# Fetched rows on partitions 32 to 127 and slots that count downwards in half of the experts, in a two-layer encoder kernel

## What is computed

```python
D_MODEL = 1024
SEQ = 256
TOP_K = 2
EXPERT_FF = 3584

def moe_swiglu(x, w_router, b_router, w1, w3, w2):
    logits = jnp.dot(t, w_router) + b_router
    top_val, top_idx = lax.top_k(logits, TOP_K)
    top_w = jax.nn.softmax(top_val, axis=-1)
    gates = jnp.sum(jax.nn.one_hot(top_idx, N_EXPERTS) * top_w[..., None], axis=1)
    for e in range(N_EXPERTS):
        he = jax.nn.silu(t @ w1[e]) * (t @ w3[e])
        out = out + gates[:, e:e + 1] * (he @ w2[e])
```

## Time and profile before

| | |
|---|---|
| median of 3 runs | 1235.1 us (1233.23 to 1238.87) |
| the profiled execution | 1235.46 us |
| its span from first to last instruction | 1233.7 us |
| granted TensorE clock, mean | 0.992 |
| TensorE busy | 93% of the span |
| bytes moved | 421.58 MB, 342 GB/s over the span |

### The profile page before, as it was taken

How to read it: one execution, slowest core, us unless ns; L and a number is a source line. 1 busy time by engine, 2 the same in 40 slices (tenths; PEclk the granted TensorE clock), 3 DMA queues, 4 the chain that set the end, 5 groups by cost and what they waited for, 6 DMA issues and landing times.

```text
span 1233.7 us, 27683 instructions
## 1 busy us (share of the span) xinstructions
PE 1149.4 (93%) x12516; PEld 682.6 (55%) x12517; DVE 325.1 (26%) x546; ACT 262.0 (21%) x402; POOL 89.8 (7%) x131
## 2 busy tenths in 40 slices
PE   8999999999999999999999978899997789999784
PEld 7888888888985446445346423334642343354232
DVE  6977766767974010000000000000100000010000
ACT  6885244345751100000000000000000000000000
POOL 5303200000001000101000100100010010001000
PEclk9999999999999999999999989999999999999998
DMA  7559565662189999999999999999999999999992
GB/s 257 191 171 331 183 202 178 197 188 85 61 311 416 421 419 376 390 405 421 425 412 423 412 408 426 419 426 410 426 410 411 427 421 421 410 425 412 427 418 95
DMA packets 75080, 421.58 MB, mean 342 GB/s; under 512 B 5906, under 2 KB 42383, under 8 KB 50384
## 3 DMA queue, kind: packets, MB, share of 16 engines
q1 hardware_dynamic: 70000, 413.16, 83.4%
q0 software_dynamic: 4960, 6.61, 2.2%
HBM read 416.54 MB, written 4.72 MB: 341 GB/s over the span
## 4 chain that ended last, share of the span: by engine, by line
PE 69%; DMA 26%; DVE 2%; ACT 1%; issue 1%; POOL 0%; POOLq 0%; SPq 0%; DVEq 0%; ACTq 0%
PE ps L1283 26%; DMA w_ring<-in_moe_w_dram 25%; PE ps L1306 14%; PE ps L1020 7%; PE ps L737 5%; PE ps L739 5%; PE ps L738 5%; PE ps L1025 3%; PE ps L1296 1%; DMA residual<-in_x_dram 0%; PE ps L858 0%; PE ps L1267 0%; POOL head_rstd L617 0%; PE ps L939 0%; PE ps L1176 0%
## 5 line engine op out<-in xcount | busy, mean ns | idle before, releaser
L1283 PE MATMUL ps<-w_ring,expert_in 128*32 128x512 f32 (+1 forms) x5120 | 496.1, 544 | 44.4 <-DMA w_ring<-in_moe_w_dram 44.4
L1283 PEld LDWEIGHTS ps<-w_ring,expert_in 128*32 128x32 f32 x5120 | 176.0, 111 | 356.2 <-issue 277.5
L1306 PE MATMUL ps<-w_ring,expert_hT 128*32 128x256 f32 x4480 | 248.7, 380 | 17.5 <-DMA w_ring<-in_moe_w_dram 17.5
L1306 PEld LDWEIGHTS ps<-w_ring,expert_hT 128*32 128x32 f32 x4480 | 144.0, 110 | 116.7 <-DMA w_ring<-in_moe_w_dram 26.5
L1790 DVE TENSOR_TENSOR w_lo<-w_raw,w_hi 128x2048 fp32r<-128x2048 f32 (+2 forms) x63 | 127.5, 2050 | 35.1 <-ACT w_hi L1367 35.0
L1020 PE MATMUL ps<-act_both,w_hi 128*128 128x512 f32 x352 | 122.4, 396 | 0.0
L1367 ACT ACTIVATE w_hi<-w_raw 128x2048 fp32r<-128x2048 f32 (+2 forms) x62 | 104.2, 1717 | 3.1 <-DMA w_raw<-in_mla_w_kvb_dram 2.4
L2351 DVE TENSOR_TENSOR expert_h<-expert_h,ps 128x896 f32<-128x896 f32 x20 | 21.8, 1088 | 301.9 <-PE ps L1283 301.8
L1025 PE MATMUL ps<-act_both,w_lo 128*128 128x256 f32 x352 | 91.4, 280 | 0.0
L1753 ACT ACTIVATE expert_hT<-ps 128x896 f32<-128x896 f32 x20 | 17.7, 916 | 284.3 <-PE ps L1296 284.3
L698 POOL DMA_INDIRECT out_dram<-expert_out,slot_row x20 | 31.1, 1554 | 592.4 <-ACT expert_out L1769 588.8
(11 more groups left out here) (357 smaller groups left out, 986.4 us busy)
## 6 DMA issues: line engine op xcount, KB each, us to landing
w_ring<-in_moe_w_dram SPq DMA_DIRECT2D x192, 1792.0 KB, 42.1
w_raw<-in_ffn_w_dram SPq DMA_DIRECT2D x33, 1024.0 KB, 5.3
w_raw<-in_lru_w_in_dram SPq DMA_DIRECT2D x8, 1024.0 KB, 5.4
w_raw<-in_mla_w_o_dram SPq DMA_DIRECT2D x4, 1024.0 KB, 5.0
w_raw<-in_lru_w_out_dram SPq DMA_DIRECT2D x4, 1024.0 KB, 5.0
w_raw<-in_mla_w_in_dram SPq DMA_DIRECT2D x8, 352.0 KB, 7.3
w_raw<-in_mla_w_qb_dram SPq DMA_DIRECT2D x4, 576.0 KB, 3.9
w_raw<-in_mla_w_kvb_dram SPq DMA_DIRECT2D x2, 1024.0 KB, 12.5
```

The costliest lines, as they stand in the source:

```text
L1283: ins = pe.matmul(ps[j * STRIP:(j + 1) * STRIP, 2 * g + b, 0:wide], in_x[:, c, k, g * STRIP:(g + 1) * STRIP], w[:, j * PART + at:j * PART ...
L1306: return pe.matmul(ps[j * STRIP:(j + 1) * STRIP, bank, at:at + DOWN_COLS], hT[:, a:a + STRIP], w, start=first and at == 0, stop=last and ( ...
```

## The change

Three things are changed.

1. The fetch has 128 rows and writes partitions 32 to 127. Partitions 0 to 31 get an offset of 1024, so their rows are out of bounds. The transposes of TensorE then have 128 rows and columns, and `take_in` reads the last 96 columns of each 128. `pick_slots` fills the token numbers with four calls rather than three, one strip further down.
2. `slot_ids` has a second version, in which the numbers of each group of 32 count downwards: 31 to 0, 63 to 32, 95 to 64. `FALLING` picks it for places 1, 2, 5 and 6. There the first token of a group sits on the last partition of a strip, for the fetch and for the adds.
3. GpSimd makes the second version and the offsets with one more iota and two more memsets.

```diff
+    FALLING = [0, 1, 1, 0, 0, 1, 1, 0]
...
-    slot_ids = sbuf.take("slot_ids", [P, CAP])
+    slot_ids = sbuf.take("slot_ids", [P, 2, CAP])
...
+            own.step(pool.iota(slot_ids[:, 1, :].rearrange("p (g t) -> p g t", g=GROUPS),
+                               pattern=[[STRIP, GROUPS], [-1, STRIP]], base=STRIP - 1, channel_multiplier=0,
+                               allow_small_or_imprecise_dtypes=True))
...
+            own.link(pool.memset(token_of[:], float(NOWHERE)))
+            own.link(pool.memset(token_of[0:STRIP, :], 2.0 * NOWHERE))
...
-                pool.indirect_dma_start(fetched_x[0:CAP, :], None, normed,
-                                        bass.IndirectOffsetOnAxis(ap=slot_token[0:CAP, c:c + 1], axis=0),
+                pool.indirect_dma_start(fetched_x[:], None, normed,
+                                        bass.IndirectOffsetOnAxis(ap=slot_token[:, c:c + 1], axis=0),
...
-                    for g in range(GROUPS):
-                        pick(g, g, SEQ + 2 * GROUPS)
+                    for j in range(STRIPS):
+                        pick(j, max(j - 1, 0), SEQ + 2 * GROUPS)
...
-                        ins = pe.transpose(ps[:, 4 + k // 4, k % 4 * CAP:(k % 4 + 1) * CAP], fetched_x[0:CAP, k * P:(k + 1) * P],
-                                           ident[0:CAP, 0:CAP])
+                        ins = pe.transpose(ps[:, 4 + k // 4, k % 4 * P:(k % 4 + 1) * P], fetched_x[:, k * P:(k + 1) * P], ident[:])
...
-                act.activation(in_x[:, c, 0:4, :], ps[:, 4, 0:4 * CAP].rearrange("p (k t) -> p k t", k=4),
+                act.activation(in_x[:, c, 0:4, :], ps[:, 4, :].rearrange("p (k t) -> p k t", k=4)[:, :, P - CAP:P],
...
-                        ins = dve.tensor_scalar(sel[:, c, i, :], slot_ids[:], sorted_rank[:, i, column(SORTED_AT[e])], None,
+                        ins = dve.tensor_scalar(sel[:, c, i, :], slot_ids[:, FALLING[e], :], sorted_rank[:, i, column(SORTED_AT[e])], None,
...
-                dve.tensor_scalar(slot_token[0:CAP, c:c + 1], ps[0:CAP, 7, at + 1:at + 2], float(NOWHERE), None,
+                dve.tensor_scalar(slot_token[:, c:c + 1], ps[:, 7, at + 1:at + 2], token_of[:, 0:1], None,
```

More of the change, by code:

```diff
@@ L240, in encoder_trunk @@
     strip_of = sbuf.take("strip_of", [P, 1])
+    token_of = sbuf.take("token_of", [P, 1])
     slot_gate = sbuf.take("slot_gate", [P, 2, GROUPS])
@@ L598, in _ @@
             own.step(pool.memset(mask[0:P // 2, P // 2:P], NEG))
-            own.step(pool.iota(slot_ids[:], pattern=[[1, CAP]], base=0, channel_multiplier=0,
+            own.step(pool.iota(slot_ids[:, 0, :], pattern=[[1, CAP]], base=0, channel_multiplier=0,
+                               allow_small_or_imprecise_dtypes=True))
+            own.step(pool.iota(slot_ids[:, 1, :].rearrange("p (g t) -> p g t", g=GROUPS),
+                               pattern=[[STRIP, GROUPS], [-1, STRIP]], base=STRIP - 1, channel_multiplier=0,
                                allow_small_or_imprecise_dtypes=True))
@@ L1213, in gather @@
                     for i in range(TT):
-                        ins = pe.matmul(ps[:, 4 + k // 4, k % 4 * CAP:(k % 4 + 1) * CAP], rx[:, i, k * P:(k + 1) * P],
+                        ins = pe.matmul(ps[:, 4 + k // 4, (k % 4 + 1) * P - CAP:(k % 4 + 1) * P], rx[:, i, k * P:(k + 1) * P],
                                         sel[:, 0, i, :], start=k % 4 == 0 and i == 0, stop=k % 4 == 3 and i == TT - 1)
@@ L2295, in _ @@
             for i in range(TT):
-                dve.tensor_scalar(sel[:, 0, i, :], slot_ids[:], rank[:, i, 0:1], None, ALU.is_equal).then_inc(sel_ready, 1)
+                dve.tensor_scalar(sel[:, 0, i, :], slot_ids[:, FALLING[0], :], rank[:, i, 0:1], None, ALU.is_equal).then_inc(sel_ready, 1)
             dve.wait_ge(top_exp, 1)
@@ L2314, in take_in @@
                 dve.tensor_copy(in_x[:, c, 4:KD, :],
-                                ps[:, 5, 0:4 * CAP].rearrange("p (k t) -> p k t", k=4)).then_inc(in_dve, 1)
+                                ps[:, 5, :].rearrange("p (k t) -> p k t", k=4)[:, :, P - CAP:P]).then_inc(in_dve, 1)
             def select(e, c, shift):
@@ L2320, in select @@
                     if shift is False:
-                        ins = dve.tensor_scalar(sel[:, c, i, :], slot_ids[:], sorted_rank[:, i, column(SORTED_AT[e])], None,
+                        ins = dve.tensor_scalar(sel[:, c, i, :], slot_ids[:, FALLING[e], :], sorted_rank[:, i, column(SORTED_AT[e])], None,
                                                 ALU.is_equal)
                     else:
-                        ins = dve.tensor_scalar(sel[:, c, i, :], slot_ids[:], top_off[:, shift], rank[:, i, column(e)],
+                        ins = dve.tensor_scalar(sel[:, c, i, :], slot_ids[:, 0, :], top_off[:, shift], rank[:, i, column(e)],
                                                 ALU.add, ALU.is_equal)
```

## The result

The changed kernel takes **1228.61 us** (median of 6 runs, 1227.14 to 1230.61) against 1235.52 us before (6 runs beside them, 1233.23 to 1239.01). The ratio is 0.9934, 95% interval 0.9920 to 0.9948, so the gain is clear and above the 0.5% that can be told. The medians differ by 6.9 us; the ratio stands for 8.2 us (6.4 to 9.9). The forecast of 1233.2 us and its range from 1229.7 us were too high. The profiled execution took 1227.14 us, its span is 1225.3 us, 8.4 us shorter than before.

What follows compares the result with a forecast made beforehand. The weight stream through full DMA engines was taken to set the end. Levelling -2.4, entries +0.2 and transposes +0.3 us made -1.9 us, giving 1233.2 us against 1235.1; range 1229.7 to 1238.2 us.

Steps and rivals of the forecast that it cites:

- What bounds the kernel: Expert part: after 507 us the DMA engines are full and the weight stream sets the end; 376 to 427 GB/s.
- 32 more entries per fetch: Each fetch: two more out-of-bounds entries per engine move no data; 0.2 us taken, between 0 and 1.2 us.
- Levelling: End of the stream: fetched rows and adds spread more evenly over DMA engines; -2.4 us taken, bounds 0 and -3.9 us.
- Levelling of the fetched rows: Seven fetches: surplus of the most loaded engine falls from 2.1 to 0.4 us; -1.7 us.
- Transposes: TensorE: 56 transposes grow to 128 x 128; 2.0 us if uncovered, mostly hidden by waits, 0.3 us taken.
- Landing and constants: A fetch landing one us later, and GpSimd's extra iota and two memsets, cost nothing.
- 1 (no change): End of the stream: slow engines are not those with many rows, only costs remain; 1235.6 us, chance 0.16.
- 2 (1226.6 us): End of the stream: small transfers are the whole cause, nearly all 10.0 us idle time goes; 1226.6 us, chance 0.07.
- 3 (the highest slots meet the slowest engine): Adds: downward counting gives the last-ending engine up to 32 more, 2.8 us; 1238.4 us, chance 0.08.
- 4 (runs of eight): Shifted fetches: shares are runs of eight, so engines 4 to 7 get 56 rows, 2.1 us more; 1237.0 us, chance 0.09.
- What would make the prediction wrong: Changed profile: end idle time stays 10.0 us, grows or shrinks to 1 or 2; `fetched_rows` waits; GB/s falls between fetches.

Runs made afterwards that it cites:

- experiment 4: Kernel before with 32 out-of-bounds entries behind the 96 of each fetch, rows on partitions 0 to 95, all slots counting upwards: 1228.23 us, ratio 0.9936.
- 5: Experiment 4 with fetches of 112 entries in place of 128: 1234.88 us, ratio 0.9986 against the kernel before.
- 6: Kernel before with fetches of 64 entries in the four places of two groups, 96 in the others: 1236.34 us, ratio 1.0000.
- experiment 1: Changed kernel with all slots counting upwards, still 128 entries and partitions 32 to 127: 1230.62 us, ratio 0.9948 against the kernel before.

## Why the prediction was wrong, point by point

- **What bounds the kernel**: right, but for the last slice, whose 95 GB/s is outside the 376 to 427 that were read. The stream sets the end, and what it gained came off the time.
- **The step that failed** is in "32 more entries per fetch": "That loss falls on all engines and comes from the rows moved, which stay the same in number." The loss was seen (366 GB/s against 427) and its cause asserted. It hangs on whether the fetch has 128 entries. With the same rows moved and 32 empty entries behind them the loss goes (experiment 4), with 16 it stays (5), and with fewer entries it is no larger (6). Its price was in the rows: 61 of 427 GB/s over 6 to 7 us is 1 us per fetch, 6 to 7 us in all. The forecast had no term for it. Two readings should have raised doubt. GB/s already holds the fetched bytes, so moving rows lowers nothing. And the adds, of 128 entries and 1024 bytes each, lose less (406) than a fetch of 96 entries of 4096 bytes. That the time still went down while the levelling brought next to nothing is the work of a term that the forecast didn't have.
- **32 more entries at 0.2 us**: no cost can be seen. A fetch of 128 costs 0.6 us, which is what its bytes take.
- **Levelling, -2.4 us**: too large, and not shown to be more than nothing. The idle time at the end fell by 0.9 us (1.6 us in the second profile), but it scatters by 0.7 us in one kernel. The direction alone gives a ratio of 0.9988, 1.5 us (0.1 to 2.7), while with 128 entries on partitions 0 to 95 mixed directions bring nothing against all upwards (0.9941 against 0.9936). "The gain is cut short by an engine that was not relieved" fits: 8 to 9 us of idle time are left, which no direction took away.
- **Levelling of the fetched rows, -1.7 us**: not borne out. Back on partitions 0 to 95 the ratio is 0.9941 with directions mixed and 0.9936 with all upwards, the same as the change within the intervals. The prediction named the rule of the Trainium skill ("DMA: Bandwidth & Descriptors", section "The descriptor swizzle") as a reason for the full 1.7 us. The runs show no such gain; which engines are slowest, on which it hangs, no view here shows.
- **Transposes, +0.3 us**: the group of the kernel after, as in the earlier trace rows, has 280 ns for one, less than the 296 ns taken:

```profile
L1274 PE MATMUL ps<-ident,fetched_rows 128*128 128x128 f32 x56 | 7.7, 280 | 0.0
```

  No wait for `fetched_rows` appeared, and a fetch lands in 10.6 us (10.7 before). Landing and constants: nothing, as forecast.
- **Rivals.** 1 (no change) fell by its time, but its reason, that levelling brings nothing, was nearer to what the runs show than the forecast's; the gain has another source. 2 (1226.6 us) came nearest in time, by luck: 9.1 us of idle time remain at the end, not 1. 3 (the highest slots meet the slowest engine) fell in part: in the change nothing got slower, but all places downwards adds 3.6 us of idle time, so the engine with the highest slots may not be far ahead of the last. 4 (runs of eight) stays open for the shift by itself: with all slots upwards the shifted kernel (experiment 1) was 2.4 us slower than kernel 4 on the same chip (1.5 us by the ratios), about the 2.1 us of this rival, but the intervals overlap; with directions mixed nothing of it is seen.
- **"What would make the prediction wrong"** named GB/s falling between fetches. It rose during them instead, and that third way, a loss that exists already and goes away, was on no list.

## What to carry to other kernels

When a small transfer runs beside a stream that fills the DMA engines, compare GB/s at equal DMA share inside and outside its window: a lower figure at share 1.0 is a loss of its own, beside its bytes, and has a price in us (missing share times length times count), as long as the stream sets the pace there. An indirect transfer of 96, 112 or 64 partitions may be worth padding to 128 with entries out of bounds, which here cost nothing that could be seen. And before a loss is called "the same as before", name the run that would take it away.

## What the runs showed of the hardware that was not expected

- A GpSimd indirect DMA of 4096-byte rows beside a stream of 128-partition loads lowers the total from 427 to a mean of 354 to 361 GB/s with 96, 112 or 64 entries, and to means of 421 to 424 with 128; the engines' share is 1.00 to 1.03 in the windows shown. So packets take longer; which ones, the views here don't tell. The Trainium skill has a rule that fits: by "DMA: Bandwidth & Descriptors", section "The descriptor swizzle", each engine of a 128-partition transfer writes through one port of SBUF, and by the section "Where 436 GB/s comes from" the 16 ports are the bottleneck. That section also has the HBM side, at about 358 GB/s for a core, bind transfers such as these; this stream moves 427, so there the measurement decides. A fetch divided otherwise would then send an engine through other engines' ports. The loss with 64, 96 and 112 entries and its absence with 128 agree with that, but no run here shows a port or how a fetch is divided, so this stays an explanation that was argued, not shown.
- The adds, 128 entries to HBM, keep their own loss, 406 and 407 GB/s in both kernels. What it comes from wasn't tried.
- The 8 to 12 us by which the mean engine ends ahead of the slowest stay open too. They are 12.0 us with all slots downwards and 8.4 to 10.7 us in the other kernels, with no order by direction or place that stands clear of scatter; the sources weren't separated.
